# An attention pipeline in a two-block transformer kernel: sums and inverses at the head of each turn, masked bias a turn ahead in two buffers, and another order of the blocks

## The reference

```
x = layer_norm(x)
h = x @ w_in + b_in            # split into qa, ka, va, qb, cb, iq, ik, iw
out_a = sliding-window attention, 8 heads, window 128, one sink each, bias by distance
out_b = attention over 8 heads on shared latents cb; each query sees only the
        top min(256, T // 4) = 128 keys by an index score, bias by distance
x = layer_norm(a * x + concat(out_a, out_b) @ w_o + b_o)
x = layer_norm(a * x + cross-attention to 256 memory rows)
x = layer_norm(a * x + square(relu(x @ w_up + b_up)) @ w_down + b_down)
```

```
score = sum_h iw[t,h] * relu(iq[t,h] . ik[s])   for s <= t, else -1e30
keep the 128 highest; p = softmax(q_lat . c[s] + bias(t - s)) over them
o = (sum_s p * c[s]) @ w_uv
```

## Time and profile before

| | us |
|---|---|
| median of three runs | 1837.8 |
| the profiled execution | 1838.7 |
| its span | 1836.9 |
| PE busy in the span | 1739.0 (95%) |
| DVE busy | 885.8 (48%) |
| ACT busy | 771.0 (42%) |
| POOL busy | 666.7 (36%) |
| mean granted clock of PE, share of full | 0.978 |

### The profile page before, as it was taken

The page is one execution under the profiler, slowest core; times in us unless marked ns, Lnnn a source line. Parts: engine busy times, 40 slices in busy tenths (PEclk is TensorE's granted clock), DMA queues, the critical chain, the costliest instruction groups (busy, mean ns, idle before and its releaser), DMA issues.

```text
span 1836.9 us, 23031 instructions
## 1 busy us (share of the span) xinstructions
PE 1739.0 (95%) x9056; PEld 1403.6 (76%) x9056; DVE 885.8 (48%) x1773; ACT 771.0 (42%) x1315; POOL 666.7 (36%) x547
## 2 busy tenths in 40 slices
PE   7999578999999999999998999999999999999998
PEld 6877356797898888887876777877788778777876
DVE  6259853443453121313656665356563453535455
ACT  5545444254353132312444555154434453434443
POOL 4634131132245444442134445534541322333330
PEclk9999699999999999999898999999999999999999
DMA  8422000121132223221122222221221211212201
GB/s 321 144 92 70 23 1 1 47 92 46 46 116 92 94 97 107 92 92 39 65 69 69 70 69 70 92 69 52 69 89 36 89 43 57 82 59 71 87 5 47
DMA packets 25812, 136.49 MB, mean 74 GB/s; under 512 B 2623, under 2 KB 7999, under 8 KB 12008
## 3 DMA queue, kind: packets, MB, share of 16 engines
q1 hardware_dynamic: 25704, 135.02, 21.6%
HBM read 132.88 MB, written 2.12 MB: 73 GB/s over the span
## 4 chain that ended last, share of the span: by engine, by line
PE 79%; DVE 12%; ACT 6%; issue 2%; DMA 0%; POOL 0%; SPq 0%; DVEq 0%; ACTq 0%
PE ps L1369 76%; PE ps L1373 2%; DVE SCB L2479 1%; DVE m L2477 1%; DVE mx L2266 1%; ACT whi L1841 1%; DVE SCB L2263 1%; ACT tmp L1841 1%; DVE LG L2263 1%; ACT L1841 1%; DVE tmp L2263 1%; ACT ESG L1841 1%; DVE GY L2263 1%; ACT ZS L1841 0%; ACT ECG L1841 0%
## 5 line engine op out<-in xcount | busy, mean ns | idle before, releaser
L2750 POOL TENSOR_TENSOR wlo<-raw,whi 128x512 fp32r<-128x512 f32 (+1 forms) x462 | 590.3, 1310 | 950.7 <-ACT whi L1841 950.7
L1369 PE MATMUL ps<-XH,whi 128*128 128x512 f32 (+1 forms) x1144 | 302.5, 384 | 9.0 <-ACT XH L1841 9.0
L1841 ACT ACTIVATE whi<-raw 128x2048 fp32r<-128x2048 f32 (+4 forms) x135 | 231.2, 1717 | 168.9 <-PE ps L1369 165.2
L1369 PE MATMUL ps<-XL,whi 128*128 128x512 f32 (+1 forms) x1144 | 281.7, 368 | 0.0
L1369 PE MATMUL ps<-XH,wlo 128*128 128x512 f32 (+1 forms) x1144 | 280.4, 367 | 0.0
L1369 PEld LDWEIGHTS ps<-XH,whi 128*128 128x128 f32 x1144 | 201.1, 191 | 55.0 <-issue 10.4
L1369 PEld LDWEIGHTS ps<-XL,whi 128*128 128x128 f32 x1144 | 204.0, 191 | 36.5
L1369 PEld LDWEIGHTS ps<-XH,wlo 128*128 128x128 f32 x1144 | 203.6, 190 | 35.5
L2355 DVE TENSOR_TENSOR R<-ps,R 128x512 f32<-128x512 f32 (+1 forms) x128 | 80.0, 625 | 274.6 <-PE ps L1369 273.9
L1369 PE MATMUL ps<-BH,whi 128*128 128x512 f32 (+1 forms) x480 | 133.1, 393 | 1.9 <-ACT BH L1841 1.9
L1369 PE MATMUL ps<-BL,whi 128*128 128x512 f32 (+1 forms) x480 | 125.7, 378 | 0.6 <-DVE BL L2678 0.6
(11 more groups left out here) (308 smaller groups left out, 2799.1 us busy)
## 6 DMA issues: line engine op xcount, KB each, us to landing
raw<-wall SPq DMA_DIRECT2D x107, 1024.0 KB, 4.7
raw<-wall SPq DMA_DIRECT2D x11, 512.0 KB, 3.5
raw<-wall SPq DMA_DIRECT2D x8, 576.0 KB, 3.6
raw<-wall SPq DMA_DIRECT2D x4, 768.0 KB, 4.1
BFL<-scr SPq DMA_DIRECT2D x2, 1024.0 KB, 6.6
outT<-R SPq DMA_DIRECT2D x16, 128.0 KB, 1.8
MEM<-memT SPq DMA_DIRECT2D x2, 512.0 KB, 5.0
XTA<-x SPq DMA_DIRECT2D x2, 512.0 KB, 9.4
```

The costliest lines, as they stand in the source:

```text
L1369: return nc.tensor.matmul(o_, l, r_, start=start, stop=stop, skip_group_check=True)
L1841: return nc.scalar.activation(o_, i_, func, bias=bias, scale=scale)
L2750: tt(wlo[u % NSPL][:, c], raw[u % NRAW][:, c], f32(whi[u % NSPL][:, c]), ALU.subtract).then_inc(S("g_lo"), 1)
```

## The change

Sums and reciprocals become a step of their own, `rd`, which is emitted for block i - 2 at the head of turn i; `rc` keeps PE's and ACT's part. The masked bias becomes a step `db` for block i + 1 behind the logits of turn i, and takes two `tmp` buffers for each block, each for two heads, in place of one for each head (blocks of n = 2 and 3). The full blocks run in the order n = 1, 2, 3, 0. Two steps of the last selection in place of four are emitted ahead of the loop, so six stand in turns 0 to 5. At the start, eight key steps in place of three are emitted ahead of the transposes of the second token half, and one in place of two ahead of each `nm` behind them.

```diff
--- before.py
+++ after.py
@@ -586,11 +586,14 @@
             nb = dsa_banks(n)
             for a in range(nb):
                 slots.append(("open", ("dl", n, g, a), "ps"))
-                if n:
-                    slots += [("open", ("db", n, g, a), "tmp"), ("close", ("db", n, g, a), [("d_lg", a + 1)])]
+                if n and (n == 1 or a % 2):
+                    slots.append(("close", ("db", n, g, a if n == 1 else a // 2), [("d_lg", a + 1)]))
                 slots.append(("close", ("dl", n, g, a), [("d_lg", a + 1)]))
             slots.append(("close", ("QL", n, g), [("p_lg", 0)]))
-            return {"p_lg": nb, "d_lg": nb, "d_sm": 2, "g_db": 4 if n else 0}, slots
+            return {"p_lg": nb, "d_lg": nb, "d_sm": 2}, slots
+
+        def masked_bias(n, g):
+            return {"g_db": 4}, [("open", ("db", n, g, i), "tmp") for i in range(2)]
 
         def key_blocks(w, n):
             return n + 1 if w == "d" else 2 if n else 1
@@ -611,7 +614,7 @@
 
         def inverses(w, n, g):
             slots = [("open", ("rc", w, n, 0 if w == "s" else g), "ps")] if w == "d" or g == 0 else []
-            signals = {"d_rd": 2 if w == "s" else 1, "p_rc": 1}
+            signals = {"p_rc": 1}
             slots.append(("close", ("mx", w, n, g), [("p_rc", 0)]))
             if w == "d" or g:
                 signals["a_rc"] = 1
@@ -728,7 +731,9 @@
             "dl": dsa_logits,
             "ex": lambda w, n, g, i: ({"a_ex": 5 if w == "s" else 2}, []),
             "tu": turns,
+            "rd": lambda w, n, g: ({"d_rd": 2 if w == "s" else 1}, []),
             "rc": inverses,
+            "db": masked_bias,
             "sv": lambda n: ({"p_sv": 1}, [("open", ("sv", n), "ps")]),
             "ss": lambda n: ({"d_ss": 1, "a_ss": 1, "g_ss": 1},
                              [("close", ("sv", n), [("d_ss", 0)]), ("close", ("ri", "s", n, 0), [("a_ss", 0), ("g_ss", 0)])]),
@@ -994,10 +999,10 @@
         emit("nm", 0, 0, 2)
         emit("ap", 0, 3)
         emit("nm", 0, 0, 3)
-        key_steps(3)
+        key_steps(8)
         emit("tp", 0, 1)
         for q in range(4):
-            key_steps(2)
+            key_steps(1)
             emit("nm", 0, 1, q)
         for i in range(8):
             key_steps(1)
@@ -1042,14 +1047,14 @@
         main_steps(1)
         index_scores(3, range(4, 8))
         last = highest(3)
-        for _ in range(4):
+        for _ in range(2):
             next(last)
         run(main)
         emit("va")
 
 
 
-        blocks = [("s", n) for n in range(4)] + [("d", n, g) for n in (3, 2, 1, 0) for g in range(2)]
+        blocks = [("s", n) for n in range(4)] + [("d", n, g) for n in (1, 2, 3, 0) for g in range(2)]
 
         def block(i):
             return blocks[i] if 0 <= i < len(blocks) else ("", 0)
@@ -1076,7 +1081,7 @@
         def each(kind, i):
             w, n, *g = block(i)
             for g_ in range(2) if w == "s" else g:
-                emit(kind, w, n, g_)
+                emit(kind, *((n, g_) if kind == "db" else (w, n, g_)))
 
         def queries(i):
             w, n, *g = block(i)
@@ -1095,7 +1100,10 @@
 
         beside = chain(*(project("wo", 4, 4) for _ in range(2)))
         for i in range(len(blocks) + 3):
+            each("rd", i - 2)
             early_logits(i)
+            if block(i + 1)[0] == "d" and block(i + 1)[1]:
+                each("db", i + 1)
             exponentials(i - 1, 0)
             each("tu", i - 2)
             scaled(i - 3)
@@ -1599,7 +1607,7 @@
             def rc(w, n, g):
                 small = slot("mx", w, n, g)
                 o_ = taken(e, "rc", w, n, 0) if w == "s" and g == 0 else slot("rc", w, n, 0) if w == "s" else taken(e, "rc", w, n, g)
-                e.wait_ge(*on("d_rd", "rc", w, n, g))
+                e.wait_ge(*on("d_rd", "rd", w, n, g))
                 if w == "s":
                     for i in range(2):
                         at_ = 128 * (2 * g + i)
@@ -2526,14 +2534,14 @@
                         tt(L[:, 2 * a:2 * a + 2, :], ps[:, 0:256].rearrange("p (i s) -> p i s", i=2), BIAS[:, h:h + 2, 128:256],
                            ALU.add).then_inc(S("d_lg"), 1)
                     elif n == 1:
-                        e.wait_ge(*on("g_db", "dl", n, g, i=2 * a + 2))
+                        e.wait_ge(*on("g_db", "db", n, g, i=2 * a + 2))
                         tt(L[:, 2 * a:2 * a + 2, :], ps[:, :].rearrange("p (i s) -> p i s", i=2),
                            slot("db", n, g, a)[:, :].rearrange("p (i s) -> p i s", i=2), ALU.add).then_inc(S("d_lg"), 1)
                     else:
                         e.wait_ge(*on("d_tk", "tk", n, 7))
                         stt(L[:, a, 0:near], ps[:, 0:near], BIAS[:, h, 0:1], SC[n - 1][:, 0:near], ALU.add, ALU.add)
-                        e.wait_ge(*on("g_db", "dl", n, g, i=a + 1))
-                        tt(L[:, a, near:N], ps[:, near:N], slot("db", n, g, a)[:, 0:256], ALU.add).then_inc(S("d_lg"), 1)
+                        e.wait_ge(*on("g_db", "db", n, g, i=a + 1))
+                        tt(L[:, a, near:N], ps[:, near:N], slot("db", n, g, a // 2)[:, 256 * (a % 2):256 * (a % 2) + 256], ALU.add).then_inc(S("d_lg"), 1)
                 softmax(L, small, "d", n, g)
 
             def tu(w, n, g):
@@ -2544,13 +2552,13 @@
                     turn_free(e, w, n, g)
                     cp(PT[:, (2 * g if w == "s" else 0) + j, :], slot("tu", w, n, g, j)[:, :]).then_inc(S("d_tu"), 1)
 
-            def rc(w, n, g):
+            def rd(w, n, g):
                 small = slot("mx", w, n, g)
                 sm, es = small[:, 8:12], small[:, 12:16]
                 e.wait_ge(*on("a_ex", "ex", w, n, g, 0 if w == "s" else 1))
                 if w == "s":
                     tt(sm, sm, es, ALU.add).then_inc(S("d_rd"), 1)
-                    e.wait_ge(*on("d_rd", "rc", w, n, g, i=1))
+                    e.wait_ge(*on("d_rd", "rd", w, n, g, i=1))
                 nc.vector.reciprocal(sm, sm).then_inc(S("d_rd"), 1)
 
             def ss(n):
@@ -2727,7 +2735,7 @@
                     e.wait_ge(*on("a_oh", "pv", p, n, i=a + 1))
                     tt(BL[:, k, :], slot("og", p, a)[:, :], f32(BH[:, k, :]), ALU.subtract).then_inc(S("d_ol"), 1)
 
-            play(dict(mem=mem, split=split, rb0=rb0, st=st_, ap=ap, nm=nm, pj=pj, bt0=bt0, ix=ix, tk=tk, sl=sl, dl=dl, rc=rc,
+            play(dict(mem=mem, split=split, rb0=rb0, st=st_, ap=ap, nm=nm, pj=pj, bt0=bt0, ix=ix, tk=tk, sl=sl, dl=dl, rd=rd,
                       tu=tu, ss=ss, ds=ds, uv=uv, cs=cs, ce=ce, ct=ct, cv=cv, dc0=dc0, dc1=dc1, sx=sx, g0=g0, g1=g1,
                       g2=g2, g4=g4, lt=lt, qk=qk, pt=pt, pv=pv))
 
@@ -2749,16 +2757,13 @@
                     e.wait_ge(*hi_of(u, n * i + n))
                     tt(wlo[u % NSPL][:, c], raw[u % NRAW][:, c], f32(whi[u % NSPL][:, c]), ALU.subtract).then_inc(S("g_lo"), 1)
 
-            def dl(n, g):
-                if n == 0:
-                    return
+            def db(n, g):
                 near = 128 * n - 128
-                nb = dsa_banks(n)
+                e.wait_ge(*on("d_tk", "tk", n, 7))
+                e.wait_ge(*on("a_bias", "rb1", 7))
                 for a in range(4):
-                    i = a % (4 // nb)
-                    buf = slot("db", n, g, a // 2) if i else taken(e, "db", n, g, a * nb // 4)
-                    e.wait_ge(*on("d_tk", "tk", n, 7))
-                    e.wait_ge(*on("a_bias", "rb1", 7))
+                    i = a % 2
+                    buf = slot("db", n, g, a // 2) if i else taken(e, "db", n, g, a // 2)
                     tt(buf[:, 256 * i:256 * i + 256], BIAS[:, 4 * g + a, :], SC[n - 1][:, near:near + 256], ALU.add
                        ).then_inc(S("g_db"), 1)
 
@@ -2782,7 +2787,7 @@
                     e.wait_ge(*on("a_gate", "gate", g))
                     tt(ec, ec, CTs[g % 2][:, cc].unsqueeze(1).to_broadcast([128, 4, 128]), ALU.mult).then_inc(S("g_ec"), 1)
 
-            play(dict(init=init, split=split, dl=dl, ss=ss, g0=g0))
+            play(dict(init=init, split=split, db=db, ss=ss, g0=g0))
 
 
         memory = memT.rearrange("(k p) t -> p k t", p=128)
```

## The result

| kernel | median, us | range | ratio to before | `OLAT` projection starts |
|---|---|---|---|---|
| before | 1838.4 (4 runs) | 1837.8 to 1839.1 | 1 | 333.55 |
| changed | 1809.5 (4 runs) | 1806.4 to 1812.6 | 0.9842 [0.9825, 0.9860] | 304.67 |
| changed, once more on another chip | 1810.8 (4 runs) | 1808.4 to 1812.6 | 0.9838 [0.9823, 0.9852] | 303.07 |

The change wins 28.9 us; 1808.2 was forecast (1801 to 1820), and the projection with `OLAT`, forecast for about 304, starts at 304.67. The four times lie in two pairs, at 1806.4 and at 1812.5, so a median between them is good to some 3 us. The profiled execution is the longest of the four, 1812.6 us, with a span of 1810.8.

What follows compares the result with a forecast made beforehand. PE, busy 95% of the span, was taken as the bound, with DVE in the attention loop's first turns. Gains 6.8 + 0 + 7.5 + 15.3 = 29.6 us from 1838.7 gave 1809.1, at the median 1808.2; range 1801 to 1820.

Steps and rivals of the forecast that it cites:

- 1. Five key steps earlier: Before the second token transposes: five more key steps fill PE's gap and move all behind it, 6.8 us gain (5.3 to 6.9).
- 2. The moved selection steps: Ahead of turn 0: DVE starts earlier but POOL holds its tiny operations, so 0 gain counted (bounds 0 and 4.5 us).
- 3. The lead, up to turn 4: Sums and inverses at the head of the turn: PE stops waiting for DVE's turn; 7.5 us gain up to turn 4.
- no wait of PE on the sums or inverses: Sign that the forecast is right: PE's waits on the inverse sums vanish from the profile; no size of its own.
- 4. Turns 4 to 14: Turn 4 to the last projection: PE's 17.7 us of waits shrink to 2.4, gain 15.3 us (bounds 10 to 17.7).
- 91.7 us are work: Turns 4 to 14: of PE's 109.4 us, all but 17.7 us of waits is work, unchanged by the block order.
- the credit given to the order of the blocks: Wide blocks d3 move to turns 8 and 9, where 2.8 us of output projection covers DVE's 5.6 us of adds and maximum.
- 5. The bias ahead: Masked bias one turn ahead on POOL: nothing gained, cost 0, up to 1.5 us if it hits DVE's tiny operations.
- A: Rival: DVE stays the bound longer, turns 3 to 9 each end 1.2 us late; 8 us less gain, 1816; chance 0.15.
- C: Rival: the early edit gives nothing, as bias copies hold banks or steps wait for weights; 6.8 us back, 1815; chance 0.12.
- B: Rival: turn 0 escapes POOL and the clock is back early; 4.5 us and 1 more, 1803; chance 0.10.
- D: Rival: slower, inverses heading DVE's queue wait for ACT's exponentials; 1841 at 4 us in eight turns; chance 0.05 with other slower ways.

Runs made afterwards that it cites:

- the run with the longer hold: The combined kernel with POOL's weight piece held until the maxima of block s1 instead of block s0: 1795.4 us, ratio 0.9758.
- the combined kernel: Changed kernel with bias in its own turn, POOL's weight piece held, queries first, three selection steps ahead of the loop, five in turns 3 to 7: 1793.1 us.

## Why the prediction was right, step by step

**1. Five key steps earlier: 6.8 us forecast, 6.77 in the trace.** The window from 37.5 to 46.1 has no gap; the next key step starts at 46.07, as before, but with five more done; the index scores start at 106.02, before at 112.79. One gap of 0.34 us on POOL's `wlo`, at 53.12, was not foreseen. Two small errors cancel here: that next key step was forecast for 46.5, so 7.2 us were gained at this place, and 0.46 of them, of which the gap may be 0.34, were gone again by the index scores. Alone the edit measured 7.2 us.

**2. The moved selection steps: 0 forecast, 0.1 in the trace** (turn 0 ends at 182.84; 189.72 less the measured shift of 6.77 is 182.95). The reason holds in its details: DVE starts early, all six tiny operations are held by POOL, 5.5 us in place of 1.0. The old order shows the same end from a start 2.4 us later, and holding POOL back shows the 3.1 us that it takes. The Trainium skill ("SBUF — State Buffer", section "Who interferes with whom") gives two rules that bear here. A DVE instruction with two SBUF inputs contends with a GpSimd one that reads SBUF; and a `tensor_scalar` in a two-port mode contends too, whoever comes first holding the ports for the whole instruction. The trace agrees with the first, and fits the second, though no row shows an instruction's mode: `TENSOR_TENSOR` and `TENSOR_SCALAR` on 128 x 4 are held until POOL's instruction (1.24 us each in the piece) ends, the maximum (177.41, where it meets POOL) keeps its 0.69 us, and the reciprocal, in the run with the longer hold, its 0.18.

**3. The lead, up to turn 4: 7.5 us forecast.** The sign "no wait of PE on the sums or inverses" was too strong: one of 6.11 us is left, in turn 2. The sum had it, though: PE was to have these inverses at 199.3, with the shift at 192.5, and has them at 192.35. The first logits of turn 4 were to start at 209.8 with the shift, and start at 209.71. Two errors cancelled here. The values of s1 start at 207.88, 1.5 us later than forecast: not for want of their copy, but because the queries ahead of them needed a PSUM bank that this copy had still to read (1.53 us at 206.32). They and the inverses, 1.6 us together, ran behind the copy, where the forecast had them ahead of it. This wait was not in my list. And they took 1.90 us where the earlier trace rows had 3.50, since PE now came to them at the higher clock; that was not safe (3.44 in the kernel with the bias in its own turn).

**4. Turns 4 to 14: 15.3 us forecast.** From 209.71 to 304.67 it is 94.96 us; 94.1 was forecast. Waits on copies: 0.93, 0.50 and 1.23, 2.66 us, against 2.4 forecast (1.7, 0 and 0.7; the last is 0.55 if turn 6's terms are added up, to 241.0 and not 241.15). Two waits were missed: 0.74 on a PSUM bank (214.83) and 0.77 on ACT's copy of the queries (236.60). That makes 4.2 us of waits, 1.8 more than forecast, and yet the stretch is only 0.9 us longer, because the term "91.7 us are work" was too large. The same stretch of turns 4 to 14 in three windows (length, PE busy, PE loads, DVE, ACT, POOL, granted clock, DMA share, GB/s), first of the kernel before:

```profile
224.13:333.55 109.42, 91.75 (x499) 65.91 (x497) 48.65 (x100) 43.30 (x119) 24.27 (x29) 0.97 0.03 10
```

then of the changed kernel, and of its repeat:

```profile
209.71:304.67 94.96, 90.79 (x498) 64.33 (x496) 58.72 (x122) 45.53 (x131) 22.46 (x27) 0.98 0.04 12
```

```profile
209.82:303.07 93.25, 89.10 (x498) 63.51 (x496) 58.52 (x122) 45.50 (x131) 22.46 (x27) 1.00 0.03 12
```

The term that was mis-sized is this one: at a granted clock of 1.00 the work is 89.1 us, not 91.7, and 2.6 us of it were stretches at the lower clock behind the waits. Half a us was what I had allowed. In the first profile 1.7 of these 2.6 are still lost, in the logits at 236.60. What failed is the credit given to the order of the blocks. I wrote that the wide blocks stand where the output projection covers DVE; the old order reaches `OLAT` at 304.02, between the changed kernel's 304.67 and 303.07. Not the order but the lead removed the waits: with the inverses out of the way, even a wide block's copy is late only once, by 2.5 us.

**5. The bias ahead: 0 forecast, with up to 1.5 us of cost.** It costs 1.3 us in turn 0, which step 2 had already counted there. No run shows a gain.

**The rivals.** A (DVE longer the bound) and C (the early edit gives nothing) did not come. (The kernel before has 3.0, 5.5, 3.7 and 5.5 us of DVE's idle time ahead of the logits of turns 4 to 7, not 5.5 in each as said against A.) B needed turn 0 to escape POOL; it takes an edit to make it do so. D names a real wait, DVE's 2.22 us for the exponentials at 237.47, but it came once, and never with a projection step's 2.8 us exceeded. In the old order such waits came three times (3.01, 2.64 and 2.64 us), and `OLAT` was not later for it. With the queries first PE's wait on their copy is gone, and DVE's is 1.68 us.

**Behind `OLAT`.** The profiled run loses 2.8 us there (1506.1 us, before 1503.4); the repeat takes 1504.0, the early edit alone 1503.4, the combined kernel 1499.1 and the one with the longer hold 1506.2. Nothing in this part was changed. Timeline of PE in the first profile:

```profile
974.56 0.66 PE L1381 MATMUL ps<-KT,XS 128*128 128x128 f32 x2 [3.66 <-ACT ZS L1849]
...
975.51 2.04 PE L1377 MATMUL ps<-XH,whi 128*128 128x512 f32 x4
```

The kernel with the longer hold has the same wait (3.67 us), and in the other profiles no wait on `ZS` is above 0.9. In the repeat PE comes to this place later, because three groups of four matmuls ahead of it ran at the lower clock (2.08, 1.91 and 1.83 us, where the first profile has 1.19, 1.08 and 1.07). So it has no wait, and its next four take 1.17 us and not 2.04. Counted from `OLAT`, the first profile is 0.6 us behind the repeat at this row and 1.9 us behind it 5 us further on. These 1.9 us and the 1.6 at `OLAT` are most of the 3.7 us between the two spans (1810.8 and 1807.1). Why the clock was low there in one run and not in the other stays open, and so does the rest of the spread: the changed kernel's eight times lie 6.3 us apart, four of them at 1812.4 to 1812.6.

**What was luck.** The forecast of 1808.2 lies within 1.3 us of the median. Steps 1, 3 and 4 each hold errors of 0.4 to 2.6 us that went against each other, and the two groups of times alone move the result by 6 us. The mechanism, the two edits and their sizes (7.2 and 24 us measured, 6.8 and 22.8 forecast) are borne out by the runs.

## What to carry to other kernels

In a software pipeline of in-order engines, put the small operation that another engine needs first at the head of the turn: 0.55 us of work moved forward (a window turn; 0.1 us in a full one) brought 24 us, and neither the order of the blocks nor the bias a turn ahead brought anything that could be seen. Before reordering large blocks, look for what the waiting engine is really behind. And where one engine is the bound (DVE in turns 0 to 2), move every optional step out of that stretch and keep POOL off it: that, with the queries first, brought another 12 us in the loop.

## What the runs showed of the hardware

**A wait costs more than itself.** From 170.7 us to `OLAT` the early edit alone and the combined kernel with the longer hold issue the same matmuls. Windows (length, PE busy, PE loads, DVE, ACT, POOL, granted clock, DMA share, GB/s):

```profile
170.70:326.54 155.84, 115.96 (x649) 83.75 (x649) 89.52 (x191) 64.37 (x194) 31.93 (x36) 0.88 0.05 16
```

```profile
170.70:291.34 120.64, 109.57 (x649) 78.21 (x649) 90.23 (x191) 64.52 (x194) 31.88 (x36) 0.96 0.05 19
```

PE is busy 6.4 us less for the same 649 records, with fewer pauses and a granted clock of 0.96 in place of 0.88, so more of them ran at the higher level (2.4 GHz): of the 35.2 us between the two, 6.4 are clock and 28.8 idle time.

**The same kernel, the same pause, another clock.** The logits at the head of turn 7 took 4.51 us (lower clock) in one profile of the changed kernel and 2.82 in the other, behind waits of the same length (1.23 or 1.24, and 0.77 us). So differences of 1 to 2 us between single profiles at `OLAT` are not to be read as an edit's.
